# Stage 3 of a hybrid diffusion layer: the activations' low parts on VectorE instead of GpSimd

## The chip, the core and the metric

The kernel runs on one core of one Trainium2 chip. The metric is device time in microseconds of one execution, the median of several runs. The engines are TensorE (PE in the profile; its weight loads are PEld), VectorE (DVE), ScalarE (ACT), GpSimd (POOL) and SyncE (SP), which here issues most DMAs. Each engine works through its own queue in order; semaphores are the only order between engines.

## The reference, cut to what matters

One layer of width 1024 for 256 prompt tokens and 2048 latent tokens, float32:

```python
h = RMSNorm(x) * (1 + scale1) + shift1
# group A: gated linear attention, 4 heads, both directions; group B: GLU, depthwise conv, LayerNorm, swish
o = rmsnorm(o_fwd + o_bwd, gla_norm_g) * silu(r)        # 512 wide
u = silu(layernorm(conv(ga * sigmoid(gg))))             # 512 wide
x = x + gate1 * (concat(o, u) @ w_out)                  # 1024 x 1024
h2 = RMSNorm(x) * (1 + scale2) + shift2
x = x + gate2 * ExpertChoiceMoE(h2)                     # router logits h2 @ w_router, 16 experts
```

The part in question is `concat(o, u) @ w_out`, with the residual and the router's logits of each token behind it.

## The kernel before, in words

**Products of float32.** TensorE's products run on operands that are split in two: a high part (the value rounded to fp32r by a copy) and a low part (value minus high part, rounded again). A product is three matmuls: high by high, high by low, low by high (helper `three`, L1651 to L1653). For the output projection the activations of one block stand in `cat_hl[:, 0]` (high) and `cat_hl[:, 1]` (low), the weights in `wo_hl`. In `cat_f(m)`, rows 0 to 3 (of 128 channels each) are the attention heads and rows 4 to 7 the conv channels.

**Stages.** Stage 1 and 2 make the projections, the scans and the convolution, and park their results in memory. Stage 3 goes over five blocks m = 0 to 4: the prompt (2 tiles of 128 tokens, `NT3[0] = 2`) and four latent blocks of 4 tiles. While PE multiplies the tiles of block m, the other engines prepare block m+1 (`prep`). Stage 4 and 5 route the tokens and run the 16 experts; they take most of the time.

**The preparation of a block.** SP loads the parked conv rows (`load_c`), attention rows (`load_o`), queries and states. VectorE runs the backward states (`back_states`, L2612, 8 chunks of 4 steps), centres the conv rows (`centre`, after PE's `conv_mean`), adds PE's inter-chunk products (`add_inter`, after `inter`, which waits for all backward states), gates the heads and inverts the roots of the statistics (`stat_recips`, L2648). PE then spreads the statistics over the partitions (`spread`, L1940), and `scale_all` on VectorE scales the four head rows (L2658) and the four conv rows (L2664).

**High and low parts.** ScalarE makes the high part of a piece, which is 4 channel rows by 128 tokens, in `cat_hi` (L1100): first the head halves of tiles 0 to 2 behind the last L2658, then silu over the four conv rows (L1093), then the conv halves of tiles 0 to 2 (`cat_his`). The two halves of tile 3 come at the start of the next block's turn, since PE must first be done with tile 3 of the block before. GpSimd makes the low parts in the same order in `cat_lo` (L1455), waiting for `r_hi` and raising `r_lo`. `piece(m, t, half)` is the count of `r_lo` at which a piece is there. PE's `out_half` waits on `r_lo` before channel row 0 and before row 4; SP's `load_c` and `load_o` for the next block wait for all pieces of the block. After block 1, GpSimd makes constants for the routing.

**Each tile g behind its product.** VectorE's `residual(g)` multiplies by the gate (two of L2679) and adds x (L2671). ScalarE takes the squares and the root (`token_stats`), VectorE inverts (`inverse`, L2686), ScalarE scales the rows (`token_rows`). PE transposes the rows (`row_T`, L1971), ScalarE evicts them (`evict`, L1133), PE multiplies by the router (`router`, L1980), VectorE copies that product out of PSUM (`logit_rows`, L2690), PE sums the four groups of it (`router_sum`, L1987; it waits for the copy), and VectorE writes the logits (`logit`, L2696).

**Order.** Every queue is written out by hand. At the end of a latent block's turn, PE has `spread(prep, g0 + 2)`, in which the second half of tile g0+2's product is interleaved with the spreads, then:

```python
router(g0 + 1)
out_half(g0 + 3, 0, 0, 4)
router_sum(g0 + 1)
out_half(g0 + 3, 0, 4, KC)
out_half(g0 + 3, 1)
row_T(g0 + 2)
```

On VectorE, `stat_recips(prep)`, `scale_all(prep)`, `residual(g0 + 2)`, `logit_rows(g0 + 1)`, `inverse(g0 + 2)` and `logit(g0 + 1)` go with these. In block 3 five rounds of the prompt's search for its routing threshold (`prompt_rounds`) stand behind `logit_rows(g0 + 1)`.

Of the kernel before, what the change touches and what calls it, by code (L numbers as in the profile page):

```python
# [24 lines left out]
NBLK = TL // BT  # L25
# [16 lines left out]
TAPS = 4 * CW  # L42
# [3 lines left out]
NT3 = [TP // 128] + [BT // 128] * NBLK  # L46
# [52 lines left out]
def hybrid_layer(nc, x_prompt, x_sample, state_gla_fwd, state_gla_bwd, c, c_ctx, norm_mix_g, norm_ffn_g,  # L99
# [3 lines left out]
    f32, f32r, bf16, u32 = mybir.dt.float32, mybir.dt.float32r, mybir.dt.bfloat16, mybir.dt.uint32  # L103
    f16 = mybir.dt.float16
    ALU = mybir.AluOpType
# [3 lines left out]
    with ctx:  # L109
# [6 lines left out]
        def sig(name, p, l=None, late=0):  # L116
            return Sig(sem(name), p, l, 0, late)
# [37 lines left out]
        def group(st, name, shape, dt=f32):  # L155
            return st.enter_context(nc.sbuf_tensor(name, shape, dt))
# [19 lines left out]
        with ExitStack() as st:  # L176
            wo_hl = group(st, "wo_hl", [128, 2, KC, D], f32r)
            work3 = group(st, "work_out", [128, WORK3])
            cat_hl = group(st, "cat_hl", [128, 2, KC, BT], f32r)
# [50 lines left out]
        def cat_f(m):  # L230
            return W3["cat"].rearrange("p (k t) -> p k t", k=KC)[:, :, 0:T3[m]]
# [129 lines left out]
        s_sg, s_u, s_conv = sig("s_sg", 4), sig("s_u", 4), sig("s_conv", TAPS)  # L361
# [7 lines left out]
        s_qst, s_sst, s_cstr = sig("s_qst", 16), sig("s_sst", 32, 16), sig("s_cstr", 16)  # L369
# [14 lines left out]
        r_T, r_hi, r_lo = s_uh.again(0), s_hhi.again(0), s_hlo.again(0)  # L384
# [10 lines left out]
        def upto(eng, sig_, n):  # L395

            eng.wait_ge(sig_.sem, sig_.base + n)

        def piece(m, t, half):

            i = 2 * half + t if NT3[m] == 2 else (3 * half + t if t < 3 else 6 + half)
            return 2 * G3[m] + i + 1
# [52 lines left out]
        def stage_end(eng, n):  # L455

            eng.drain().then_inc(s_ph, 1)
            eng.wait_ge(s_ph, 5 * n)
# [909 lines left out]
        def _(pool):  # L1368
# [84 lines left out]
            def cat_lo(m, t, half):  # L1453
                upto(pool, r_hi, piece(m, t, half))
                pool.tensor_tensor(cat_hl[:, 1, 4 * half:4 * half + 4, 128 * t:128 * t + 128],  # L1455
                                   cat_f(m)[:, 4 * half:4 * half + 4, 128 * t:128 * t + 128],
                                   cat_hl[:, 0, 4 * half:4 * half + 4, 128 * t:128 * t + 128].bitcast(f32),
                                   ALU.subtract).then_inc(r_lo.sem, 1)

            p, first, final = Blk(), Blk(0), Blk(NBLK - 1)  # L1460
# [44 lines left out]
                                         (pr_id[:, :, :], [[128, 2], [0, 2]], 1)):  # L1505
                    chain(pool.iota(out, pattern, base=0, channel_multiplier=cm, allow_small_or_imprecise_dtypes=True))

            for m in range(NBLK + 1):
                for half in range(2):
                    if m == 0:  # L1510
                        final.wait(pool, s_conv if half == 0 else s_cstr, TAPS if half == 0 else s_cstr.l)
                    for t in range(min(NT3[m], 3)):
                        cat_lo(m, t, half)
                if NT3[m] == 4:
                    cat_lo(m, 3, 0)
                    cat_lo(m, 3, 1)
                if m == 1:
                    routing_constants()
            stage_end(pool, 2)
            last_stores(pool)  # L1520
            n_c = [N_CONST]
# [809 lines left out]
        def _(dve):  # L2331
# [24 lines left out]
            p, first, final = Blk(), Blk(0), Blk(NBLK - 1)  # L2356
# [267 lines left out]
            def centre(m):  # L2624
                dve.wait_ge(r_me, m + 1)
                for ct in range(4):
                    x = cat_f(m)[:, 4 + ct, :]
                    dve.scalar_tensor_tensor(out=x, in0=psum[6][:, 0:T3[m]], scalar=-1.0 / 512, in1=x, op0=ALU.mult,
                                             op1=ALU.add).then_inc(r_xc, 1)
# [15 lines left out]
            def stat_recips(m):  # L2645
# [4 lines left out]
                dve.tensor_tensor(spread_rs[64:128, 0:T3[m]], rs, spread_rs[0:64, 0:T3[m]].bitcast(f32), ALU.subtract)\  # L2650
                   .then_inc(r_sl.sem, 1)

            def scale_all(m):
                for h in range(H):
                    dve.wait_ge(r_bc, 5 * m + h + 1)
                    dve.wait_ge(r_or, 4 * m + h + 1)
                    o = cat_f(m)[:, h, :]
                    dve.scalar_tensor_tensor(out=o, in0=o, scalar=col[:, V_GN:V_GN + 1], in1=psum[6 + h % 2][:, 0:T3[m]],  # L2658
                                             op0=ALU.mult, op1=ALU.mult).then_inc(r_on, 1)
                dve.wait_ge(r_bc, 5 * m + 5)  # L2660
                dve.wait_ge(r_csq, 4 * m + 4)
                for ct in range(4):
                    x = cat_f(m)[:, 4 + ct, :]
                    dve.tensor_tensor(x, x, psum[6][:, 0:T3[m]], ALU.mult).then_inc(r_cn, 1)  # L2664

            def residual(g, rounds=0):
                residual_half(g, 0)
                prompt_rounds(rounds)
                residual_half(g, 1)
                dve.wait_ge(r_y, 2 * g + 2)  # L2670
                dve.tensor_tensor(x3[:, g % 2, :], x3[:, g % 2, :], xn3[:, g % 2, :], ALU.add).then_inc(r_x2, 1)  # L2671
# [16 lines left out]
            def logit_rows(g):  # L2688
                dve.wait_ge(r_ro, 4 * g + 4)
                dve.tensor_copy(lgT[:, g % 2, :], psum[5][:, 0:128]).then_inc(r_lt.sem, 1)  # L2690
# [9 lines left out]
            def prologue():  # L2700
                dve.tensor_tensor(spread_sel[:, 0:H], ident[:, 32:32 + H], ident[:, 96:96 + H], ALU.add)
                dve.tensor_tensor(spread_sel[:, H:H + 1], ident[:, 0:1], ident[:, 64:65], ALU.add)
                dve.memset(W3["wrA"][:, 2 * KC * NE:2 * KC * NE + NE], 0.0)
                dve.tensor_reduce(selg, ident[:, :].rearrange("p (g c) -> p c g", g=4)[:, 0:NE, :], AX.X, ALU.add)
                dve.wait_ge(s_vec2, 16)
                for c in range(2):
                    dve.tensor_tensor(wrA[:, c], wr[:, :, :], A2[:, :, c:c + 1].broadcast_to([128, KC, NE]),
                                      ALU.mult).then_inc(r_wr, 1)

                def wo_lo(k):  # L2710
                    dve.wait_ge(r_wh, k + 1)
                    dve.tensor_tensor(wo_hl[:, 1, k, :], wstage[k // 2 % 3][:, k % 2, :], wo_hl[:, 0, k, :].bitcast(f32),
                                      ALU.subtract).then_inc(r_wl, 1)

                centre(0)
                taps(final, LATE, 118)
                add_inter(0)
                taps(final, 118, TAPS)
                wo_lo(0)
                wo_lo(1)  # L2720
                wo_lo(2)
                wo_lo(3)
                gate_heads(0)
                wo_lo(4)
                wo_lo(5)
                stat_recips(0)
                wo_lo(6)
                wo_lo(7)
                scale_all(0)
                dve.wait_ge(r_br, 1)  # L2730
                dve.tensor_copy(brow_w, psum[5][:, 0:2 * NE]).then_inc(r_wr, 1)

            def stage3(m):
                g0, prep = G3[m], m + 1 if m < NBLK else None
                if m > 0:
                    residual(g0 - 1)
                if prep is None:
                    last_tiles(g0)
                    return
                back_states(prep, 0, 3)  # L2740
                if m > 0:
                    inverse(g0 - 1)
                if m > 1:
                    logit_rows(g0 - 2)
                back_states(prep, 3, 5)
                if m > 1:
                    logit(g0 - 2)
                back_states(prep, 5, NC3[prep])
                centre(prep)
                if m > 0:  # L2750
                    logit_rows(g0 - 1)
                add_inter(prep, (0, 1))
                if m > 0:
                    logit(g0 - 1)
                residual(g0)
                inverse(g0)
                add_inter(prep, (2, 3))
                gate_heads(prep)
                if NT3[m] == 2:
                    stat_recips(prep)  # L2760
                    logit_rows(g0)
                    logit(g0)
                    scale_all(prep)
                    return
                residual(g0 + 1)
                logit_rows(g0)
                if m == 1:
                    prompt_shift()
                if m == 2:
                    prompt_softmax()  # L2770
                if m == 3:
                    prompt_columns()
                inverse(g0 + 1)
                logit(g0)
                stat_recips(prep)
                scale_all(prep)
                residual(g0 + 2)
                logit_rows(g0 + 1)
                if m == 3:
                    prompt_rounds(5)  # L2780
                inverse(g0 + 2)
                logit(g0 + 1)
# [95 lines left out]
            for m in range(NBLK + 1):  # L2878
                stage3(m)
# [391 lines left out]
```

## Time and profile before

| | us |
|---|---|
| median of 3 runs | 2388.03 |
| lowest, highest | 2385.71, 2391.93 |
| profiled execution | 2388.8 |
| span of its trace | 2387.1 |

In the profiled execution TensorE is busy for 2228.6 us of the span, VectorE for 1668.1, ScalarE for 1193.4 and GpSimd for 722.5. Stage 3 lies between about 714 and 1055 us; its first output matmul starts at 750.2, its last at about 1047. A busy time says how long an engine had an instruction in execution, and not that it set the pace. That is read from the waits: which engine stood idle, and which other's semaphore it was waiting for. In a timeline row, `xN` merges N instructions of one kind in a row, and the bracket holds the idle time before the first of them.

### The profile page before, as it was taken

To read this page: it belongs to the slowest core of one execution; us is meant where nothing else is said; L and a number is where in the kernel's file an instruction comes from. 1 tells how busy PE (TensorE), PEld (TensorE's weight loads), DVE (VectorE), ACT (ScalarE), POOL (GpSimd) and SP (SyncE) were. 2 spreads that over 40 slices of the span, in tenths; PEclk is the share of its full clock that TensorE was granted. 3 is DMA by queue.
4 is the path that set the end of the run, shared out by engine and by line. 5 is a ranking of instruction groups with operands and counts; after the bars stand their busy time and mean duration, and the time that the engine had idled before them with its cause. 6 is when DMAs were issued, how large, how long until landed. Compare 5 with 4: busy or idle time off the path is not lost.

```text
span 2387.1 us, 43833 instructions
## 1 busy us (share of the span) xinstructions
PE 2228.6 (93%) x16687; PEld 2049.2 (86%) x16687; DVE 1668.1 (70%) x2936; ACT 1193.4 (50%) x1935; POOL 722.5 (30%) x664
## 2 busy tenths in 40 slices
PE   4789999999997899976999999999999999999995
PEld 4778888888785677753999999999999999999995
DVE  2879989898888766767666656566566656666585
ACT  3765473644434454423545554555545554555574
POOL 2000000000000311101254455544554455534451
PEclk8999999999998999987999999999999999999998
DMA  8986676767737566264576677766776677766986
GB/s 292 358 295 214 231 254 240 247 201 260 236 124 240 186 198 200 99 176 132 170 210 189 178 208 199 207 185 184 208 205 193 179 202 199 211 183 186 299 253 242
DMA packets 289653, 505.79 MB, mean 212 GB/s; under 512 B 26177, under 2 KB 232894, under 8 KB 273920
## 3 DMA queue, kind: packets, MB, share of 16 engines
q1 hardware_dynamic: 249622, 376.39, 48.3%
q0 software_dynamic: 39424, 126.64, 19.5%
q8 instruction: 78, 1.28, 0.2%
q10 hardware_dynamic: 490, 1.16, 0.1%
q14 instruction: 39, 0.32, 0.0%
HBM read 405.61 MB, written 98.53 MB: 211 GB/s over the span
## 4 chain that ended last, share of the span: by engine, by line
PE 61%; DVE 4%; DMA 2%; ACT 1%; issue 1%; POOL 0%; SPq 0%; DVEq 0%; POOLq 0%; ACTq 0%
PE bank L1651 19%; PE bank L1653 19%; PE bank L1652 19%; DMA out_dram<-work_exp 1%; PE bank L1905 1%; PE bank L1971 1%; DVE work_exp L2922 1%; PE bank L1915 1%; PE bank L1923 1%; DVE work_exp L3185 0%; PE bank L2142 0%; PE bank L1980 0%; POOL cat_hl L1455 0%; DMA work_exp<-x_rows 0%; DMA park_s<-work_proj 0%
## 5 line engine op out<-in xcount | busy, mean ns | idle before, releaser
L1651 PE MATMUL bank<-act_hl_exp,hl_exp 128*128 128x288 f32 x3072 | 909.5, 296 | 11.3 <-DVE hl_exp L3101 7.4
L1652 PE MATMUL bank<-act_hl_exp,hl_exp 128*128 128x288 f32 x3072 | 907.1, 295 | 0.0
L1653 PE MATMUL bank<-act_hl_exp,hl_exp 128*128 128x288 f32 x3072 | 905.5, 295 | 0.0
L1651 PEld LDWEIGHTS bank<-act_hl_exp,hl_exp 128*128 128x128 f32 x3072 | 577.2, 188 | 12.3 <-DVE hl_exp L3101 8.9
L1653 PEld LDWEIGHTS bank<-act_hl_exp,hl_exp 128*128 128x128 f32 x3072 | 579.2, 189 | 0.0
L1652 PEld LDWEIGHTS bank<-act_hl_exp,hl_exp 128*128 128x128 f32 x3072 | 577.9, 188 | 0.0
L3101 DVE TENSOR_TENSOR hl_exp<-work_exp,hl_exp 128x1024 fp32r<-128x1024 f32 x192 | 231.4, 1227 | 205.4 <-ACT hl_exp L1231 205.4
L3101 DVE TENSOR_TENSOR hl_exp<-raw_exp,hl_exp 128x1024 fp32r<-128x1024 f32 x192 | 232.2, 1225 | 192.5 <-ACT hl_exp L1231 192.4
L2561 DVE SCALAR_TENSOR_TENSOR work_proj<-work_proj,wcv 128x392 f32<-128x392 f32 (+12 forms) x600 | 338.9, 636 | 1.2
L1231 ACT ACTIVATE hl_exp<-work_exp 128x1024 fp32r<-128x1024 f32 x192 | 199.2, 1054 | 201.2 <-PE bank L1653 201.2
L1231 ACT ACTIVATE hl_exp<-raw_exp 128x1024 fp32r<-128x1024 f32 x192 | 198.5, 1052 | 160.7 <-PE bank L1653 160.7
L1566 POOL TENSOR_TENSOR act_hl_exp<-work_exp,act_hl_exp 128x288 fp32r<-128x288 f32 x128 | 155.6, 1234 | 359.4 <-ACT act_hl_exp L1257 359.4
L1589 POOL DMA_INDIRECT x_rows<-work_exp x135 | 241.6, 1790 | 60.3 <-issue 36.0
L1651 PE MATMUL bank<-act_hl_proj,hl_proj 128*128 128x512 f32 (+1 forms) x640 | 236.5, 370 | 6.0 <-DVE hl_proj L2388 6.0
L1653 PE MATMUL bank<-act_hl_proj,hl_proj 128*128 128x512 f32 (+1 forms) x640 | 233.1, 364 | 0.0
L1652 PE MATMUL bank<-act_hl_proj,hl_proj 128*128 128x512 f32 (+1 forms) x640 | 233.0, 364 | 0.0
L1428 POOL DMA_DIRECT2D hl_proj<-park_w x80 | 42.8, 536 | 589.5 <-PE bank L1653 500.8
L1554 POOL DMA_INDIRECT work_exp<-h_rows,work_exp x135 | 161.3, 1195 | 50.0 <-issue 38.3
L1242 ACT ACTIVATE work_exp<-work_exp 128x256 f32<-128x256 f32 x240 | 102.3, 497 | 90.3 <-DVE work_exp L3112 67.0
L1651 PEld LDWEIGHTS bank<-act_hl_proj,hl_proj 128*128 128x128 f32 x640 | 121.7, 190 | 25.8 <-issue 7.6
L1653 PEld LDWEIGHTS bank<-act_hl_proj,hl_proj 128*128 128x128 f32 x640 | 121.6, 190 | 19.1
L1652 PEld LDWEIGHTS bank<-act_hl_proj,hl_proj 128*128 128x128 f32 x640 | 121.8, 190 | 17.9
(412 smaller groups left out, 3315.5 us busy)
## 6 DMA issues: line engine op xcount, KB each, us to landing
hl_proj<-park_w POOLq DMA_DIRECT2D x80, 1024.0 KB, 6.4
raw_exp<-in_w_e_gate_dram SPq DMA_DIRECT2D x32, 1024.0 KB, 5.9
raw_exp<-in_w_e_up_dram SPq DMA_DIRECT2D x32, 1024.0 KB, 5.8
work_exp<-in_w_e_gate_dram SPq DMA_DIRECT2D x32, 1024.0 KB
work_exp<-in_w_e_up_dram SPq DMA_DIRECT2D x32, 1024.0 KB, 6.0
raw_exp<-in_w_e_down_dram SPq DMA_DIRECT2D x32, 1024.0 KB, 6.2
work_exp<-in_w_e_down_dram SPq DMA_DIRECT2D x32, 1024.0 KB, 5.7
park_w<-hl_proj SPq DMA_DIRECT2D x8, 2048.0 KB, 12.2
```

What stands on the lines that cost most here:

```text
L1231: act.activation(half_out(j, q, 0, is_last(e)), half_in(src, j, q, is_last(e)), ACT.Copy).then_inc(s_hi, 1)
L1242: last = act.activation(h32e[:, k % 2, a:z], xT[:, k % 2, a:z], ACT.Identity, scale=A2q[:, cnd, k:k + 1], bias=sh2q[:, cnd, k:k + 1])
L1428: pool.dma_start(hl[:, j % 2, q], park_w[j, :, q]).then_inc(s_w[j % 2][q].sem, 16)
L1554: pool.indirect_dma_start(xg[:, b, :], None, h2_rows[:, :], bass.IndirectOffsetOnAxis(ap=ids_g[:, b:b + 1], axis=0)).then_inc(e_gat, 16)
L1566: pool.tensor_tensor(xe_hl[:, 1, k, :], h32e[:, k % 2, :], xe_hl[:, 0, k, :].bitcast(f32), ALU.subtract)\
L1589: pool.indirect_dma_start(x2_quarters[:, :], bass.IndirectOffsetOnAxis(ap=ids_s[:, b:b + 1], axis=0), y_t[:, b, :], None, compute_op=ALU.a ...
L1651: pe.matmul(out, lh, rh, start=first, stop=False)
L1652: pe.matmul(out, lh, rl, start=False, stop=False)
L1653: return pe.matmul(out, ll, rh, start=False, stop=last_)
L1905: ins = pe.matmul(psum[7 - h % 2][v:v + 64, 64 * cc:64 * cc + 64], S3[:, cc + 1, 128 * h + v:128 * h + v + 64], part("q", m, h)[:, 64 * cc ...
L2561: dve.scalar_tensor_tensor(out=ac[:, :, a0:a1], in0=uu[:, :, a0 + off:a1 + off], scalar=wcv[:, ct, w:w + 1], in1=ac[:, :, a0:a1], op0=ALU. ...
L3101: dve.tensor_tensor(half_out(j, q, 1, is_last(e)), half_in(src, j, q, is_last(e)), half_out(j, q, 0, is_last(e)).bitcast(f32), ALU.subtrac ...
```

## The change

All 36 subtractions of `cat_lo` leave GpSimd's queue and become `low_rows` on VectorE, with the same waits on `r_hi`, the same operands and the same raising of `r_lo`, in the same order of pieces. Their places in VectorE's queue:

- block 0, in the prologue: the two head pieces behind `scale_all(0)`, the copy of L2731, then the two conv pieces;
- block 1: the three head pieces behind `scale_all(1)`, which ends the turn of block 0; the three conv pieces at the start of the turn of block 1, ahead of `residual(1)`; the two pieces of tile 3 behind that residual;
- blocks 2 to 4: the three head pieces behind `scale_all(prep)` and ahead of `residual(g0 + 2)`; the three conv pieces behind that residual and ahead of `logit_rows(g0 + 1)`; the two pieces of tile 3 behind the next `residual`.

GpSimd waits for the third conv piece of block 1 and then makes the routing constants, which came behind all pieces of block 1 before. It does nothing else in stage 3.

```diff
--- before.py
+++ after.py
@@ -1505,17 +1505,8 @@
                                          (pr_id[:, :, :], [[128, 2], [0, 2]], 1)):
                     chain(pool.iota(out, pattern, base=0, channel_multiplier=cm, allow_small_or_imprecise_dtypes=True))
 
-            for m in range(NBLK + 1):
-                for half in range(2):
-                    if m == 0:
-                        final.wait(pool, s_conv if half == 0 else s_cstr, TAPS if half == 0 else s_cstr.l)
-                    for t in range(min(NT3[m], 3)):
-                        cat_lo(m, t, half)
-                if NT3[m] == 4:
-                    cat_lo(m, 3, 0)
-                    cat_lo(m, 3, 1)
-                if m == 1:
-                    routing_constants()
+            upto(pool, r_lo, piece(1, 2, 1))
+            routing_constants()
             stage_end(pool, 2)
             last_stores(pool)
             n_c = [N_CONST]
@@ -2650,6 +2641,15 @@
                 dve.tensor_tensor(spread_rs[64:128, 0:T3[m]], rs, spread_rs[0:64, 0:T3[m]].bitcast(f32), ALU.subtract)\
                    .then_inc(r_sl.sem, 1)
 
+            def low_rows(m, t, half):
+                upto(dve, r_hi, piece(m, t, half))
+                if m == 0 and t == 0 and half == 1:
+                    final.wait(dve, s_cstr, s_cstr.l)
+                k0, k1 = 4 * half, 4 * half + 4
+                dve.tensor_tensor(cat_hl[:, 1, k0:k1, 128 * t:128 * t + 128], cat_f(m)[:, k0:k1, 128 * t:128 * t + 128],
+                                  cat_hl[:, 0, k0:k1, 128 * t:128 * t + 128].bitcast(f32), ALU.subtract)\
+                   .then_inc(r_lo.sem, 1)
+
             def scale_all(m):
                 for h in range(H):
                     dve.wait_ge(r_bc, 5 * m + h + 1)
@@ -2727,13 +2727,22 @@
                 wo_lo(6)
                 wo_lo(7)
                 scale_all(0)
+                low_rows(0, 0, 0)
+                low_rows(0, 1, 0)
                 dve.wait_ge(r_br, 1)
                 dve.tensor_copy(brow_w, psum[5][:, 0:2 * NE]).then_inc(r_wr, 1)
+                low_rows(0, 0, 1)
+                low_rows(0, 1, 1)
 
             def stage3(m):
                 g0, prep = G3[m], m + 1 if m < NBLK else None
+                if m == 1:
+                    for t in range(3):
+                        low_rows(1, t, 1)
                 if m > 0:
                     residual(g0 - 1)
+                    low_rows(m, 3, 0)
+                    low_rows(m, 3, 1)
                 if prep is None:
                     last_tiles(g0)
                     return
@@ -2761,6 +2770,8 @@
                     logit_rows(g0)
                     logit(g0)
                     scale_all(prep)
+                    for t in range(3):
+                        low_rows(prep, t, 0)
                     return
                 residual(g0 + 1)
                 logit_rows(g0)
@@ -2774,7 +2785,11 @@
                 logit(g0)
                 stat_recips(prep)
                 scale_all(prep)
+                for t in range(3):
+                    low_rows(prep, t, 0)
                 residual(g0 + 2)
+                for t in range(3):
+                    low_rows(prep, t, 1)
                 logit_rows(g0 + 1)
                 if m == 3:
                     prompt_rounds(5)
```

## Rows read from the trace of the kernel before

**Rows 1.** The page, part 1: busy us (share of the span) and count of each engine.
```profile
PE 2228.6 (93%) x16687; PEld 2049.2 (86%) x16687; DVE 1668.1 (70%) x2936; ACT 1193.4 (50%) x1935; POOL 722.5 (30%) x664
```

**Rows 2.** Busy time, count by engine, then TensorE's granted clock, DMA share, GB/s in two stretches.
```profile
792.10:802.40 10.30, 7.69 (x15) 4.56 (x15) 9.90 (x15) 7.99 (x13) 5.15 (x5) 0.50 0.88 225
...
802.40:1048.00 245.60, 244.31 (x1643) 185.13 (x1643) 164.26 (x417) 109.05 (x174) 47.09 (x74) 1.00 0.50 161
```

**Rows 3.** Waits in 745:1050: engine, line waited for; us in total, times, longest.
```profile
PE bank L1651 <- POOL cat_hl L1455: 4.6, 3, 2.0
...
PE bank L1987 <- DVE keep L2690: 3.6, 5, 2.3
```

**Rows 4.** Groups of VectorE instructions in 745:1050: count, busy us, mean ns, idle before.
```profile
L2643 DVE TENSOR_TENSOR work_out<-work_out 128x512 f32<-128x512 f32 x16 | 10.0, 687 | 2.4 <-ACT work_out L1074 2.4
...
L2658 DVE SCALAR_TENSOR_TENSOR work_out<-work_out,col,bank 128x512 f32<-128x512 f32 x16 | 11.6, 746 | 7.0 <-PE bank L1940 6.9
```

**Rows 5.** Instructions on the tile cat_hl: duration ns min/median/max, first and last start.
```profile
L1100 ACT ACTIVATE cat_hl<-work_out x36: 612/618/636, 748.0 to 996.9; 128x512 fp32r<-128x512 f32 x36
L1455 POOL TENSOR_TENSOR cat_hl<-work_out,cat_hl x36: 1263/1298/1403, 748.8 to 998.4; 128x512 fp32r<-128x512 f32 x36
```

**Rows 6.** Timeline of PE: start us, us, what, [idle before it, releaser].
```profile
750.21 0.77 PE L1651 MATMUL bank<-wo_hl,cat_hl 128*128 128x512 f32 x1 [1.98 <-POOL cat_hl L1455]
```

**Rows 7.** Timeline of VectorE before stage 3's first output matmul.
```profile
748.27 1.41 DVE L2664 TENSOR_TENSOR work_out<-work_out,bank 128x256 f32<-128x256 f32 x4 [0.28 <-PE bank L1940]
```

**Rows 8.** Timeline of VectorE around the start of m = 1.
```profile
794.47 2.48 DVE L2664 TENSOR_TENSOR work_out<-work_out,bank 128x512 f32<-128x512 f32 x4
...
800.39 8.63 DVE L2612 SCALAR_TENSOR_TENSOR work_out<-work_out,dec 64x128 f32<-64x128 f32 x12
...
809.24 3.79 DVE L2612 SCALAR_TENSOR_TENSOR work_out<-work_out,dec 64x128 f32<-64x128 f32 x12
```

**Rows 9.** Timeline of ScalarE, same stretch.
```profile
800.30 2.71 ACT L1100 ACTIVATE cat_hl<-work_out 128x512 fp32r<-128x512 f32 x5
```

**Rows 10.** Timeline of PE, same stretch.
```profile
796.48 0.77 PE L1651 MATMUL bank<-wo_hl,cat_hl 128*128 128x512 f32 x1 [2.05 <-POOL cat_hl L1455]
...
802.47 0.50 PE L1651 MATMUL bank<-wo_hl,cat_hl 128*128 128x512 f32 x1 [0.53 <-POOL cat_hl L1455]
...
812.38 3.70 PE L1915 MATMUL bank<-work_out,ones 128*128 128x512 f32 x8 [0.41 <-DMA work_out<-park_c]
...
816.59 0.63 PE L1905 MATMUL bank<-work_out 128*64 128x64 f32 x14
```

**Rows 11.** Timeline of SyncE's queue, same stretch.
```profile
807.66 0.33 SPq L645 DMA_DIRECT2D work_out<-park_c  x1
```

**Rows 12.** Timeline of VectorE at the end of m = 1.
```profile
849.90 2.48 DVE L2664 TENSOR_TENSOR work_out<-work_out,bank 128x512 f32<-128x512 f32 x4 [0.89 <-PE bank L1940]
852.30 1.28 DVE L2679 TENSOR_TENSOR work_out<-bank,work_out 128x512 f32<-128x512 f32 x2
853.61 1.23 DVE L2671 TENSOR_TENSOR work_out<-work_out 128x1024 f32<-128x1024 f32 x1
854.76 0.28 DVE L2690 COPY keep<-bank 128x128 f32<-128x128 f32 x1
```

**Rows 13.** Timeline of ScalarE, same stretch.
```profile
856.27 1.67 ACT L1100 ACTIVATE cat_hl<-work_out 128x512 fp32r<-128x512 f32 x3
```

**Rows 14.** Timeline of PE, same stretch and block 2.
```profile
855.10 0.40 PE L1987 MATMUL bank<-work_out,keep 128*128 128x16 f32 x2 [0.27 <-DVE keep L2690]
...
873.57 0.39 PE L1653 MATMUL bank<-wo_hl,cat_hl 128*128 128x512 f32 x1
873.80 0.29 PE L1987 MATMUL bank<-work_out,keep 128*128 128x16 f32 x2
```

**Rows 15.** Timeline of ScalarE at the start of m = 2.
```profile
867.40 1.14 ACT L1100 ACTIVATE cat_hl<-work_out 128x512 fp32r<-128x512 f32 x2
```

**Rows 16.** Timeline of VectorE at the start of m = 2.
```profile
865.98 0.42 DVE L2606 COPY work_out<-carry 64x512 f32<-64x512 f32 x1
```

## The prediction

> **What bounds the kernel now.** I read the page first, then the stretches of stage 3, then who waits for whom there, and last the timelines of single engines around each wait. The page has TensorE (PE) busy for 93% of the span [rows 1]. From 802.4 to 1048 us, which is nearly all of stage 3, it is busy 244.3 of 245.6 us at the full granted clock [rows 2]; so in stage 3 a microsecond counts only where PE itself stands still, and its order of work is fixed. The list of waits names what it stands still for: the low parts that GpSimd makes, 4.6 us in three waits, and VectorE's copy of the router's rows, L2690, 3.6 us in five [rows 3]. The first is what the change touches. The second is where I expect its price.
>
> **What is moved.** The 36 subtractions of L1455 leave GpSimd (1.30 us each) [rows 5] and become 36 on VectorE. The trace has no such subtraction there at this shape. The nearest are L2643, 128x512 with both inputs in SBUF, 0.687, and L2658, the dearest of that size, 0.746 [rows 4]; four of L2664 in a row take 2.48, so 0.60 from start to start with 0.68 for the last [rows 8]. I take 0.60 in a row and 0.69 for the last, which is L2643's; the ends are 0.60 and 0.75. VectorE has room for 36 x 0.60 = 22 us, PE being the bound. What matters is what stands behind each one in VectorE's queue, since each waits for ScalarE's high part.
>
> **Start of m = 0.** PE's first output matmul waits for GpSimd until 750.21 [rows 6]. Now the piece comes behind the four half-width scalings that end at 748.27 + 1.41 = 749.68 [rows 7], and is there at 750.3. Cost 0.1 (0 to 0.7).
>
> **Start of m = 1.** Head rows stand behind all scalings, the conv ones included. These end at 794.47 + 2.48 = 796.95 [rows 8], the first piece at 797.55, PE starts at 797.6 instead of 796.48 [rows 10]: +1.1. Twelve matmuls take 802.47 - 0.53 - 796.48 = 5.46 [rows 10], to 803.1, where it met the next wait and went on at 802.47. The conv piece it needs there is ready by 801.65: ScalarE's first conv part starts at 800.30 [rows 9] and takes 0.62 [rows 5], then 0.69. So PE is 0.6 late. The next VectorE work follows: third conv piece until 802.7, the residual of tile 1 (two of 0.60 and one of 1.23) until 805.2, the pieces of tile 3 until 806.4. SP's loads of the next conv and head rows wait for that last piece; they left at 807.66 behind GpSimd [rows 11] and leave 1.2 earlier, so PE's 0.41 for park_c goes [rows 10]. PE reaches conv_mean 0.2 late.
>
> Behind it VectorE runs the backward states, 32 steps of L2612. They started at 800.39 and start at 806.8, six microseconds later. Half of it comes back: the first twelve took 8.63 us while GpSimd was subtracting, the next twelve 3.79 after it [rows 8]. With 0.316 each all 32 take 10.1, and end at 817.1 with the reciprocal between. PE wants them at 816.59 + 0.2 [rows 10]: it waits 0.3. For m = 1 that is +0.5 in all (0 to 2).
>
> On the slow steps, the Trainium skill (SBUF — State Buffer, "SBUF: two separate sides") says that a VectorE operation with two SBUF inputs and a GpSimd operation share a port pair by an exclusive lock, and the loser blocks for the whole instruction. The trace agrees: 8.63 against 3.79, while L2664, one input in PSUM, keeps its 0.68 beside GpSimd's pieces. By the rule VectorE gets this time back in every block; were the slow steps due to something else, that is the last rival.
>
> **The price: router_sum.** In blocks m = 1, 2, 3 the new order on VectorE is: scalings, three head pieces, residual(g0+2), three conv pieces, and only then logit_rows(g0+1), the copy L2690. PE's queue has router(g0+1), twelve matmuls of out_half(g0+3), then router_sum(g0+1), which reads that copy; everything of PE stands behind it. Before, the copy ran from 854.76 to 855.04 and PE waited 0.27, until 855.10 [rows 12, 14]. Now:
> - three head pieces: the residual's first part moves from 852.30 by 3 x 0.60, its last ends at 853.61 + 1.23 + 1.8 = 856.65 [rows 12];
> - the conv pieces wait for ScalarE, which first applies silu to what the conv scalings of 849.90 leave [rows 12]; its three conv parts run from 856.27 for 1.67, until 857.94 [rows 13]. Nothing of the change moves them;
> - the third conv piece runs from 857.98 to 858.67, the copy from 858.6 to 858.9, and PE resumes at 858.9.
>
> PE loses 858.9 - 855.1 = 3.8 us. There is nothing to absorb it, as PE was 99.5% busy [rows 2] and can't take other work first. The same three rows recur, with the same distances within 0.1, at 920.25 and 985.66; block 4 has no scalings and last_tiles doesn't have this order. Three times 3.8 is 11.5 us. The ends are 5.4, if only the three head pieces of 0.60 counted, and 13, with pieces of 0.75 from start to start (the residual then ends at 857.1, the third conv piece at 859.35, which is 4.4 a time).
>
> **The clock.** The twelve matmuls of 5.46 us ran at 1.2 GHz [rows 2, 10]; at 2.4 GHz they start 0.23 apart [rows 14], and twelve take 3.0 with the last one's tail. In stage 3 both starts after PE had stood still for some 2 us or more run at half clock: 0.50 was granted from 792.1 to 802.4, with PE busy 7.69 [rows 2]. The 0.3 us waits later brought no fall. A stop of 4.1 us (3.8 and the old 0.27) is longer than these, so I expect 1.2 GHz for a few microseconds behind each. Twelve matmuls at half clock lose 5.46 - 3.0 = 2.4; I take 2.0, since part of the stretch will lie in the stop itself. The ends are 0 (no fall) and 3.8 (half of 7.69). Three times 2.0 is 6.0.
>
> The Trainium skill (TensorE: Matmul & The Clock Gate, "What's actually happening") says that the throttled state is the default and activity releases it. That is in line with the granted 0.50 there. Were the clock to hold through such a stop, the sum would be that of the first rival.
>
> **The rest.** In block 2 VectorE's two pieces of tile 3 wait for ScalarE's of 867.40, that end at 868.54 [rows 15]; they are done at 869.3 and the states' first copy starts then, not at 865.98 [rows 16]. Copy 0.42, twelve steps 3.8 and the reciprocal bring the copy L2690 to 873.8 to 874.1, PE wants it at 873.80 [rows 14]: 0.2, and less later, where ScalarE has no exponential ahead. The states end ahead of conv_mean. GpSimd's constants start 4 us earlier and are needed only after stage 3: nothing. The prompt's search rounds lose GpSimd as a neighbour, but sit where PE doesn't wait.
>
> **Sum.** 0.1 + 0.5 + 11.5 + 6.0 + 0.2 = 18.3 us. The profiled execution took 2388.8, its span 2387.1; so 2407.1. The median of the runs shown lies 0.8 lower, hence 2406.3.
>
> **Rivals.**
> - *The clock holds.* The waits come as above, but 2.4 GHz stays granted: 12.3, 2400.3. For it: a single stop with full work on both sides, where both old falls had several. Against: the length. 0.12.
> - *Faster: PE's waits for low parts vanish.* GpSimd's 1.30 becomes 0.69, the three waits of 4.6 us [rows 3], the 0.41 and the slow matmuls behind both starts (2.4 each) go: 9.8 less, 2378.2. It decides if the conv scalings don't stand ahead of the first head piece and the copy L2690 comes before PE has done its twelve matmuls. The order in the code has both the other way, and the first wait can shrink by 0.6 at most. 0.04.
> - *No change, 2388.* The pieces fill VectorE's idle time and PE doesn't notice. For it: VectorE is busy 164 of 245.6 us [rows 2]. Against: the copy follows straight on the residual [rows 12], so no idle time lies ahead of it. 0.04.
> - *The states stay slow.* If what slows L2612 is not GpSimd, the 32 steps take 5 us longer in block 1 and up to 2 in blocks 2 and 3; PE waits 5 more at inter and 1 later, with another 2 of clock: 2414 to 2415. 0.08.
> - The forecast: 0.72, own range 2402 to 2411.
>
> **The numbers.** About 0.3%, 7 us, is what a measurement of this kernel tells from no change. The range reaches down to just below the first rival, 2399, and up to the last, 2414. Slower by over 7 us: 0.90 (forecast, holding clock, slow states). Within: 0.06. Faster: 0.04.
>
> **What would show it.** The waits after: PE for DVE L2690 near 12 us instead of 3.6, none for GpSimd; three idle times of 4 us on PE, some 65 us apart; a granted clock below 1.00 behind each; L2612 with no member over 0.5 us; PE's first matmul of m = 1 1.1 us later. I am wrong if PE's idle time before router_sum stays at 0.3, or if PE's wait at L1905 grows to several microseconds.

## The result, and the profile after

The changed kernel takes 2411.24 us (median of 6 runs, 2405.46 to 2414.71) against 2389.35 before (6 runs): a ratio of 1.0093, 95% interval 1.0083 to 1.0104, so 20 to 25 us more. The forecast was 2406.3 in a range of 2399 to 2414, slower with 0.90. Its direction, its mechanism and its places held; the size, 18.3 us for 21.9, came out 16% low, and the time lies just above the narrower range of 2402 to 2411 that the forecast gave for itself.

The page after, first line of part 1, and the granted clock of part 2, a digit for each fortieth of the span:

```profile
PE 2240.8 (93%) x16687; PEld 2060.8 (85%) x16687; DVE 1675.7 (69%) x2972; ACT 1193.2 (49%) x1935; POOL 677.8 (28%) x628
...
PEclk8999999999997999996999999999999999999998
```

VectorE has 36 instructions more and GpSimd 36 less than in [rows 1]. Yet VectorE is busy only 8 us longer, where 36 x 0.69 are 25; below, much of the rest turns out to be what GpSimd's subtractions had cost it. PE is busy 12 us longer with the same 16687 matmuls. That is no work, but the same work at a lower clock.

Two stretches after: the half-clock start of m = 1, and from its end to stage 3's last output matmul (busy us and count of PE, PEld, DVE, ACT, POOL; then granted clock, DMA share, GB/s). They answer to [rows 2].

```profile
796.20:806.40 10.20, 6.83 (x16) 4.83 (x16) 7.85 (x14) 8.59 (x13) 0.41 (x2) 0.50 0.79 208
806.40:1069.80 263.40, 249.99 (x1626) 189.79 (x1625) 172.56 (x448) 108.34 (x172) 12.47 (x43) 0.96 0.47 150
```

PE stood still for 1.3 of 245.6 us before. Now it stands still for 13.4 of 263.4, and the mean clock is 0.96 where it was 1.00. The waits of PE in stage 3 after (us in total, times, longest), against [rows 3]:

```profile
PE bank L1978 <- DVE keep L2690: 16.1, 6, 4.3
...
PE bank L1642 <- DVE cat_hl L2649: 5.5, 2, 3.3
...
PE bank L1896 <- issue: 0.6, 1, 0.6
```

(L1978 is the old L1987, router_sum; L1642 the old L1651; L2649 is the new subtraction, L1896 the first inter product.) The wait for the copy L2690 grew from 3.6 to 16.1. The one for low parts, the change's subject, grew too, from 4.6 to 5.5.

The end of m = 1 on VectorE, ScalarE and PE, against [rows 12 to 14]:

```profile
853.45 2.48 DVE L2664 TENSOR_TENSOR work_out<-work_out,bank 128x512 f32<-128x512 f32 x4 [0.88 <-PE bank L1931]
855.85 1.89 DVE L2649 TENSOR_TENSOR cat_hl<-work_out,cat_hl 128x512 fp32r<-128x512 f32 x3
857.66 1.28 DVE L2679 TENSOR_TENSOR work_out<-bank,work_out 128x512 f32<-128x512 f32 x2
858.98 1.23 DVE L2671 TENSOR_TENSOR work_out<-work_out 128x1024 f32<-128x1024 f32 x1
860.49 1.89 DVE L2649 TENSOR_TENSOR cat_hl<-work_out,cat_hl 128x512 fp32r<-128x512 f32 x3 [0.28 <-ACT cat_hl L1100]
862.30 0.28 DVE L2690 COPY keep<-bank 128x128 f32<-128x128 f32 x1
```

```profile
859.82 1.67 ACT L1100 ACTIVATE cat_hl<-work_out 128x512 fp32r<-128x512 f32 x3
```

```profile
862.64 0.61 PE L1978 MATMUL bank<-work_out,keep 128*128 128x16 f32 x2 [4.26 <-DVE keep L2690]
...
866.64 0.63 PE L1644 MATMUL bank<-wo_hl,cat_hl 128*128 128x512 f32 x1
867.07 0.63 PE L1642 MATMUL bank<-wo_hl,cat_hl 128*128 128x512 f32 x1
...
868.12 0.39 PE L1642 MATMUL bank<-wo_hl,cat_hl 128*128 128x512 f32 x1
868.35 0.39 PE L1643 MATMUL bank<-wo_hl,cat_hl 128*128 128x512 f32 x1
```

The order is read off line by line: scalings, three head pieces, residual, a short wait for ScalarE's first conv part at 859.82, three conv pieces, and then the 0.28 us copy for which PE had stood still since 858.38. Behind the stop the matmuls start 0.43 apart, and 0.23 apart from 867.9. The same stop comes at 934.29 and 1006.07:

```profile
934.29 0.61 PE L1978 MATMUL bank<-work_out,keep 128*128 128x16 f32 x2 [4.26 <-DVE keep L2690]
```

```profile
1006.07 0.61 PE L1978 MATMUL bank<-work_out,keep 128*128 128x16 f32 x2 [4.25 <-DVE keep L2690]
```

**Where the time went.** From stage 3's first output matmul to its last, the traces have 1047.09 - 750.21 = 296.9 us before and 1069.82 - 752.68 = 317.1 after: +20.3. I use this length below, since it leaves out how early stage 3 begins, which moves by up to 4 us between profiles of kernels that are alike up to there. It divides into:

| term | forecast | measured |
|---|---|---|
| three stops, each grown from 0.27 to 4.26 | 11.5 | 12.0 |
| half clock behind the three | 6.0 | 7.1 |
| start of m = 0 | 0.1 | 0.7 |
| start of m = 1 | 0.5 | 0.4 |
| copy L2690 in block 2 | 0.2 | 0 |
| sum | 18.3 | 20.2 |

The clock term is read from the distance between router_sum's start and that of row_T, in the traces before and after:

```profile
863.79 1.03 PE L1971 MATMUL bank<-ident,work_out 128*128 128x128 f32 x8
```

```profile
873.70 0.49 PE L1962 MATMUL bank<-ident,work_out 128*128 128x128 f32 x3
```

That is 863.79 - 855.10 = 8.69 and 873.70 - 862.64 = 11.06; over the three blocks the growth is 2.37, 2.38 and 2.34. The start of m = 0 is a term apart. The first output matmul's own wait, which the 0.1 was for, lies ahead of this length; the 0.7 is slow matmuls behind it, and kernels with the old start of m = 0 show it too.

### The profile page after: what moved, and what is told of

Its sections match the earlier page's. It is cut to its first block, busy times and chain, and to the rows that moved or that the text cites. A ratio compares the mean times of both kernels' runs of the same rounds, so it can differ in the third digit from the quotient of the medians.

```text
span 2412.9 us, 43831 instructions
## 1 busy us (share of the span) xinstructions
PE 2240.8 (93%) x16687; PEld 2060.8 (85%) x16687; DVE 1675.7 (69%) x2972; ACT 1193.2 (49%) x1935; POOL 677.8 (28%) x628
## 4 chain that ended last, share of the span: by engine, by line
PE 62%; DVE 4%; DMA 2%; ACT 1%; issue 1%; SPq 0%; POOL 0%; DVEq 0%; ACTq 0%; POOLq 0%
PE bank L1642 19%; PE bank L1644 19%; PE bank L1643 19%; DMA out_dram<-work_exp 1%; PE bank L1896 1%; PE bank L1962 1%; DVE work_exp L2937 1%; PE bank L1906 1%; PE bank L1914 1%; DVE work_proj L2552 0%; DVE work_exp L3200 0%; DMA work_exp<-x_rows 0%; PE bank L2133 0%; PE bank L2205 0%; PE bank L1971 0%
## 5 line engine op out<-in xcount | busy, mean ns | idle before, releaser
L1642 PE MATMUL bank<-act_hl_exp,hl_exp 128*128 128x288 f32 x3072 | 909.9, 296 | 12.3 <-DVE hl_exp L3116 8.7
L1642 PEld LDWEIGHTS bank<-act_hl_exp,hl_exp 128*128 128x128 f32 x3072 | 577.7, 188 | 13.0 <-DVE hl_exp L3116 10.2
L1642 PE MATMUL bank<-act_hl_proj,hl_proj 128*128 128x512 f32 (+1 forms) x640 | 237.0, 370 | 6.0 <-DVE hl_proj L2379 6.0
L1642 PEld LDWEIGHTS bank<-act_hl_proj,hl_proj 128*128 128x128 f32 x640 | 122.1, 191 | 25.8 <-issue 7.6
```

What stands on the lines that cost most here:

```text
L1642: pe.matmul(out, lh, rh, start=first, stop=False)
```

## The experiments

All were timed in five rounds beside the kernel before. "Length" is that of the output matmuls, as above. The next two ask whether it is the order, or VectorE's added load.

**x1: the copy first.** All low parts stay on VectorE.

```diff
                 scale_all(prep)
+                logit_rows(g0 + 1)
                 for t in range(3):
                     low_rows(prep, t, 0)
                 residual(g0 + 2)
                 for t in range(3):
                     low_rows(prep, t, 1)
-                logit_rows(g0 + 1)
```

> All 36 low parts stay on VectorE; only the copy logit_rows(g0+1) moves, from behind the three conv pieces to right behind scale_all(prep). Order theory: PE's three stops of 4.3 us before router_sum go, the half-clock stretches behind them too, and of the 22 us only the later start of m = 0 and 1 is left (1.3), less the old 0.28 three times: +0.5 us against before, 2390. Rival, VectorE's added 24 us of work are themselves the price (it becomes the bound or fights over SBUF): most of the 22 us stays, 2405 or more.

Measured: 2390.5 us, ratio 1.0004 (0.9995 to 1.0013), length 296.9, within 0.01 of the kernel before: the starts of m = 0 and 1 cost 0.8 more, and the three stops of 0.27 are gone. Its waits and the stretch behind m = 1's start:

```profile
PE bank L1978 <- DVE keep L2690: 3.3, 3, 2.3
```

```profile
806.90:1052.00 245.10, 243.53 (x1644) 185.20 (x1642) 173.60 (x451) 108.73 (x173) 12.86 (x45) 1.00 0.51 162
```

Moving one instruction of 0.28 us takes the whole cost away, with VectorE carrying all 36 pieces. The load isn't the price; the rival falls.

**x3: PE asks later.** VectorE's queue is the changed one.

```diff
-                out_half(g0 + 3, 0, 0, 4)
-                router_sum(g0 + 1)
-                out_half(g0 + 3, 0, 4, KC)
-                out_half(g0 + 3, 1)
+                out_half(g0 + 3, 0)
+                out_half(g0 + 3, 1, 0, 4)
+                router_sum(g0 + 1)
+                out_half(g0 + 3, 1, 4, KC)
```

> VectorE's queue as in the changed kernel, the copy still 7 us late; only PE's queue differs: router_sum(g0+1) stands behind 36 matmuls of tile g0+3 instead of 12. Order theory: PE reaches it 24 x 0.23 = 5.6 us later, at 864.0 on the changed kernel's clock where the copy is there at 862.6, so no stop and no fall of the clock: +1 us against before, 2390. Rival, VectorE's load or the late copy itself costs (inverse and logit behind it come later, x2 and h2 go out later): 2400 or more.

Measured: 2390.0 us, ratio 1.0010 (1.0001 to 1.0019), length 297.1, no stop at router_sum in blocks 1 to 3. So the copy may come as late as in the changed kernel; it costs only because PE's queue asks for it after twelve matmuls.

**x4 and x5: the change in halves.** In x4 VectorE makes the pieces of blocks 0 and 1, in x5 those of 2 to 4; GpSimd makes the others, in the old order.

```diff
 def low_rows(m, t, half):
+    if m not in (0, 1):      # x5: (2, 3, 4)
+        return
```

> VectorE makes the low parts of blocks 0 and 1 alone, GpSimd those of blocks 2 to 4 as before. Order theory: only the terms of the starts of m = 0 and m = 1, +1.3 us, with PE's stops before router_sum at 0.28 again: 2390 to 2391. A rival that puts the cost on the starts (PE's first matmul of m = 1 waits 3.3 us for VectorE) would leave 5 us or more here.

> The other half: GpSimd makes the low parts of blocks 0 and 1 as before, VectorE those of blocks 2 to 4 in the changed kernel's places. Order theory: three stops, each 4.0 us longer than before, and 2.4 us of half clock behind each, 19 us: 2408. With x4 the two add up to the change's 22 within 3 us; if they don't, the halves act on each other.

Measured: x4 2390.8 us, 1.0008 (0.9999 to 1.0017), length 297.7 (+0.9); x5 2409.7, 1.0082 (1.0068 to 1.0096), length 317.2 (+20.3), with stops of 4.25, 4.26 and 4.25. The price sits in the second half. The two add up to 21.2 in length, with 20.3 for both at once, so neither depends on the other. (In x5 the first half-clock stretch and the conv wait of m = 1 came out 0.7 us longer than in the profile of before, with the same work there; terms under 1 us at the starts are at that level.)

**x7: the wait alone.** The kernel before, with nothing moved:

```diff
                 residual(g0 + 2)
+                upto(dve, r_hi, piece(prep, 2, 1))
                 logit_rows(g0 + 1)
```

> The kernel before, all low parts on GpSimd; one wait added on VectorE: logit_rows(g0+1) waits for ScalarE's third conv high part of the next block. Nothing is moved to VectorE. Order theory: the copy runs from 858.0 to 858.3 instead of 854.8 to 855.0, PE's stop grows by 3.2 us and the clock falls behind it by 2.4: 3 x 5.6 = 16.8 us, 2406. Rival, the cost comes with VectorE's extra work: near 0.

Measured: 2406.5 us, 1.0075 (1.0061 to 1.0089), length 313.1 (+16.2). The copy waits for ScalarE's third conv part and PE for the copy:

```profile
859.73 0.29 DVE L2690 COPY keep<-bank 128x128 f32<-128x128 f32 x1 [3.13 <-ACT cat_hl L1100]
```

```profile
860.07 0.61 PE L1987 MATMUL bank<-work_out,keep 128*128 128x16 f32 x2 [3.49 <-DVE keep L2690]
```

Of the 22 us, 16 to 18 come without a single subtraction on VectorE. So most of the price is that the copy was put behind ScalarE's silu chain; the pieces add the last 0.8 us of each stop and about 1 us of half clock in all.

**x2: the copy between.** As x1, but the copy stands behind the head pieces and the residual, ahead of the conv pieces.

> All low parts on VectorE; the copy logit_rows(g0+1) stands behind the three head pieces and residual(g0+2) but ahead of the three conv pieces. Order theory: the copy comes 1.8 us late instead of 7.5 - 3.5 = 4.0, so three stops of 2.1 us. Whether the clock falls behind a stop of 2.1 us is what this one asks: without a fall 3 x 1.8 + 1.3 - 0 = 6.7 us more than before, with one each time 13.9: 2396 or 2403. I expect some of the three to fall: 2399.

Measured: 2398.8 us, 1.0043 (1.0029 to 1.0056), length 306.5 (+9.7), three stops of 2.07:

```profile
857.70 0.40 PE L1978 MATMUL bank<-work_out,keep 128*128 128x16 f32 x2 [2.07 <-DVE keep L2690]
```

Three times 1.8 and the 1.1 of the starts are 6.5; the other 3.1 are clock. It was granted at half for 3.4 us behind the first two stops, where the distance from router_sum to row_T grew by 1.54 and 1.56, and not at all behind the third, where it stayed 8.70.

**x6: the stop filled.** The changed kernel, with matmuls for PE to do while it is late. They are extra work whose results nobody reads.

```diff
                 out_half(g0 + 3, 0, 0, 4)
+                pe.wait_ge(r_on, 4 * prep + 4)
+                for i in range(16):
+                    pe.matmul(psum[7][:, :], wo_hl[:, 0, i % 8, 0:128],
+                              wo_hl[:, 0, i % 8, 0:512], start=True, stop=True)
                 router_sum(g0 + 1)
```

> The changed kernel with 16 matmuls of 128x512 whose results nobody reads, on a bank that is free, between the twelve matmuls and router_sum(g0+1) in m = 1 to 3: PE is late as before, but works through 3.7 of the 4.3 us. Clock theory: the half-clock stretches at those places go and with them 2.4 us each, so 7 us less than the changed kernel: +15 us against before, 2404. Rival, the 2.4 us are not the clock but the pile-up of waits behind the stop: no gain against the changed kernel, 2411.

Measured: 2402.3 us, 1.0055 (1.0042 to 1.0069), length 309.4, which is 7.7 less than the changed kernel, though router_sum comes as late:

```profile
854.70 3.83 PE L2058 MATMUL bank<-wo_hl 128*128 128x512 f32 x16
859.13 0.40 PE L1978 MATMUL bank<-work_out,keep 128*128 128x16 f32 x2 [0.60 <-DVE keep L2693]
```

```profile
802.00:1060.00 258.00, 255.08 (x1693) 194.13 (x1691) 173.59 (x451) 108.97 (x173) 12.86 (x45) 1.00 0.48 154
```

The clock stays at 1.00 over the stretch, and the distance from router_sum to row_T is 8.70, 8.70 and 8.69 again. The second term, 7.1 us, is thereby shown to be the clock and not a pile-up behind the stop. (The other 0.6 of the 7.7 lies at the start of m = 0, where half clock lasted 4.2 us behind the first output matmul and not 5.9.)

**x8 to x10: a faster kernel?** x8 is x1 with the first head piece of blocks 0 and 1 between the conv scalings. x9 adds sixteen idle matmuls at the start of m = 1, ten before router_sum(0) and six behind the spreads; x10 adds nine and three more at the start of m = 0. `keep_busy(n, ...)` is a wait for the free bank and n matmuls of 128x512 into it.

```diff
                     dve.tensor_tensor(x, x, psum[6][:, 0:T3[m]], ALU.mult).then_inc(r_cn, 1)
+                    if (m, ct) in ((0, 1), (1, 0)):
+                        low_rows(m, 0, 0)
...
                     router(g0)
+                    keep_busy(10, r_y, 2)       # x9
                     router_sum(g0)
                     spread(prep)
+                    keep_busy(6, r_y, 2)        # x9
```

> x1 with the first head piece of block 0 and of block 1 put between the conv scalings (behind the second and behind the first of them), so PE can start sooner. By rows: start of m = 0 0.3 us earlier, m = 1's first matmul 0.6 earlier than before, but its fifth row still waits for the conv piece, which is 0.6 later: 0.1 gained; PE's 0.41 for park_c and 3 x 0.28 before router_sum gone. Sum -1.5 us against before: 2388, not distinguishable from it. Rival: the held-back conv rows cost more than the head piece gives: +1 or more.

> x8 with 16 matmuls of 128x512 whose results nobody reads at the start of m = 1: ten ahead of router_sum(0), where PE stood still for 2.34 us, and six behind the spreads, where it stood still for 1.5 to 3.3. Clock theory: the fall to half clock there (10.2 us of it, PE busy 7.7) goes and up to 3.8 us come back: the time from the first to the last output matmul goes from x8's 296.1 to 293, the median to 2386 against 2388.7 of before. Rival, the stretch is not due to these stops, or the fillers hold up real work: 296 or more, no gain.

> x9 with twelve more such matmuls at the start of m = 0, nine ahead of spread(0) (PE stood still for 2.3 to 4.0 us there) and three behind it. Clock theory: part of the half-clock stretch under the first output matmuls (4 to 6 us) goes: 1 to 2 us less than x9, 2384. Rival: there the clock is low well before, the fillers run at half speed and delay spread(0) and with it VectorE's scalings: 1 to 2 us more than x9.

Measured: x8 2389.9 us, 1.0005 (0.9996 to 1.0014), length 296.1. x9 2386.8, 0.9986 (0.9977 to 0.9995), length 297.0. x10 2387.0, 0.9991 (0.9983 to 1.0000), length 296.8. In x9 the fall of the clock at m = 1 is gone, and still the length isn't shorter:

```profile
793.00:806.00 13.00, 8.95 (x36) 5.97 (x35) 10.08 (x18) 8.60 (x13) 0.61 (x3) 1.00 0.83 204
```

```profile
798.13 0.48 PE L1642 MATMUL bank<-wo_hl,cat_hl 128*128 128x512 f32 x1 [0.29 <-DVE cat_hl L2656]
...
803.98 0.50 PE L1642 MATMUL bank<-wo_hl,cat_hl 128*128 128x512 f32 x1 [2.81 <-DVE cat_hl L2656]
```

```profile
799.61 2.93 ACT L1093 ACTIVATE work_out<-work_out,col 128x512 f32<-128x512 f32 x4
802.57 2.71 ACT L1100 ACTIVATE cat_hl<-work_out 128x512 fp32r<-128x512 f32 x5
```

PE does its twelve matmuls at full clock and then waits 2.81 us for the conv piece, which hangs on ScalarE's silu. The whole lengths of x8 and x9 can't be compared for this: behind the first output matmul, ahead of x9's fillers, half clock happened to last 3.2 us in x8 and 5.8 in x9. From the last output matmul of m = 0 to the first of m = 2 it is 77.44 us in x8 and 77.15 in x9. So the slow clock at m = 1 had cost 0.3 us, because it ran beside that chain, and not the predicted 3. In x10 the clock was at half for 5.6 us behind the first output matmul; without its fillers this lasts 3.2 to 6.2, so no gain shows. x9's median is 0.14% below the kernel before, with the interval just clear of 1; its profile doesn't show where from, and I don't claim a cause.

## Why the prediction was right

- **The copy before router_sum.** Right, in place, order and size: 3.8 us forecast, 4.0 measured, three times. x1 and x3 each undo one end of the dependence and bring the length back to that of before. The missing 0.2 us is in the conv pieces: they began with ScalarE's first part, and three in a row at 0.60 ended after its third, where I had let the third piece wait for the third part alone. The stops come 71.7 us apart and not 65, since each block also grows by its own stop and slow matmuls.
- **ScalarE sets it, not the work moved.** x7 shows it. The forecast had said that nothing of the change moves those parts; they start 3.55 us later in the trace after, exactly as much as the scalings ahead of them.
- **The clock.** Right in kind; 2.0 was too small, it is 2.4 behind a stop of 4.3 us, the very figure that the twelve matmuls of [rows 10] had given before I took something off it. That the two figures meet is luck, since the twelve don't say how long this stretch lasts. The trace after has 0.50 for 6.8 us at each stop, and the first 1.6 to 1.7 of them lie in the stop itself, as I had said; what I had too short was the whole stretch. The first rival, a clock that holds, is out: at stops of this length it held only where PE was kept at work (x6). That goes with the Trainium skill (TensorE: Matmul & The Clock Gate, "What's actually happening"): activity releases the throttle.
- **The start of m = 0.** Its first matmul waited 2.20 instead of 1.98 us, 0.2 for the 0.1 forecast, but the half clock lasted until 758.6, 5.9 us behind the first matmul, and not 4.4 as before, which is the 0.7 of the table. x5 and x7, whose start of m = 0 is that of before, have 6 us of it too: this length varies by itself, and the forecast has no term for it.
- **The start of m = 1.** First matmul held back by 1.2 more (1.1 forecast), the two later waits gone, and 0.64 new ahead of `inter` (0.3 forecast). The profile names no releaser for it, but the last backward step ended at 820.08 and PE went on at 820.18, so I read it as the wait for the states. The length grew by 0.4 there, for 0.5 forecast.
- **The slow states.** The last rival is out. VectorE's subtractions on cat_hl and the backward steps after (duration in ns, min/median/max):

```profile
L2649 DVE TENSOR_TENSOR cat_hl<-work_out,cat_hl x36: 683/685/783, 751.9 to 1020.4; 128x512 fp32r<-128x512 f32 x36
```

```profile
L2603 DVE SCALAR_TENSOR_TENSOR work_out<-work_out,dec x128: 346/355/399, 757.3 to 959.7; 64x128 f32<-64x128 f32 x128
```

  The subtraction costs 0.685, as its nearest row said. With GpSimd's subtractions away no backward step takes over 0.40 us. All 128 are busy for 37.2 us, where they were for 48.6 before, and for 41.3 and 43.4 in x4 and x5, where GpSimd keeps part of the pieces. So VectorE did get its time back, and nothing came of it, since PE was the bound.
- **No change, and faster.** Both are out. The forecast named 12 us for this copy in the list of waits after. It is 16.1: 12 is only the growth, and waits that the change leaves alone, the longest 2.34 us in block 0, stand in both lists.

**Open.** The medians differ by 21.9 us, the lengths by 20.3; the rest is inside the interval. x3 and x4 also have medians 1 to 2 us above before with lengths within 1 us of it. No profile shows a place for that.

## What to carry to other kernels

When work is moved into another engine's queue, price what stands behind it there, not the work: here 25 us of subtractions were free and a 0.28 us copy behind them cost 20. Look for the shortest instruction in that queue that the bounding engine asks for soon, and put it ahead of anything that waits for a third engine. A stop of TensorE of some 2 us or more can cost more than its length, because slow matmuls follow it, unless another chain is the bound just there.

## What the runs showed of the hardware

- **Stops of PE and the half clock behind them.** With full work on both sides, two of three stops of 2.07 us were followed by 3.4 us at 0.50, costing 1.54 and 1.56, and one by none (x2). Stops of 3.49 us cost 1.6, 1.6 and 3.0 (x7), those of 4.26 us 2.4 each, with 6.8 us at 0.50, and 2.4 to 2.8 in x5. Behind 0.60 and 0.27 there was none (x6, before). So behind a stop of about 2 us the fall came or stayed out, and these runs don't show on what that hangs; at the nine stops of 3.49 us and more it was there every time.
- **A short VectorE step beside a long GpSimd one.** A backward step of 64x128 takes 0.355 us. In the kernel before, of the twelve that took 8.63 us [rows 8] five took 1.26 to 1.39 us each, while GpSimd made five subtractions in a row, so a run of short steps goes at the pace of these; an operation with one input in PSUM kept its 0.68. Not every work of GpSimd does this, as one would think from the prediction's sentence on the shared ports: its next instructions lie beside the twelve steps of [rows 8] that took 3.79 us.

```profile
808.18 4.47 POOL L1486 TENSOR_SCALAR_AFFINE_SELECT work_exp<-work_exp 128x128 bf16<-128x128 bf16 x8
```

  Before, the 23 steps beside such selects alone took 0.35 us in the median and 0.45 at most; after, 28 steps beside them took 0.40 at most.
